# An attention, convolution, expert and MLP model on one core: the order of the first norm tile and kv products, a wait on GpSimd, and twenty-four extra TensorE products

## The reference

```python
def rmsnorm(x, g):
    xf = x * lax.rsqrt(jnp.mean(x * x, axis=-1, keepdims=True) + NORM_EPS)
    return xf * g
...
h = rmsnorm(x, norm1_g)
q, k, v, gate_b, gate_c, xc, ... = split(h @ w_in)     # 512, 128, 128, 512, 512, 512, ...
...
# c_layer of the second block: three branches over the same queries
out = gate0 * o_compressed + gate1 * o_selected + gate2 * o_window
```

## Time and profile before

| | us |
|---|---|
| median of 3 runs | 1994.71 (1994.18 to 1997.05) |
| the profiled execution, its own time | 1996.16 |
| its span, from first to last instruction | 1994.4 |
| TensorE busy in the span | 1874.3 (94%) |
| mean granted TensorE clock | 0.981 |

### The profile page before, as it was taken

The page is one execution under the profiler, slowest core; times in us unless marked ns, Lnnn a source line. Parts: engine busy times, 40 slices in busy tenths (PEclk is TensorE's granted clock), DMA queues, the critical chain, the costliest instruction groups (busy, mean ns, idle before and its releaser), DMA issues.

```text
span 1994.4 us, 28241 instructions
## 1 busy us (share of the span) xinstructions
PE 1874.3 (94%) x11002; PEld 1467.3 (74%) x11002; DVE 1025.2 (51%) x2029; ACT 815.9 (41%) x1551; POOL 565.5 (28%) x401
## 2 busy tenths in 40 slices
PE   6999999998778999988999999999899999999998
PEld 5878889832223893457988888899767798888886
DVE  4170443521113625873376676822567625676777
ACT  4122651311012413364554544353366636544443
POOL 4244431011110420144421123233045643113211
PEclk8999999999889999999999999999889999999999
DMA  6222403799999330201123223321203012223321
GB/s 236 86 85 86 168 1 149 267 401 419 421 420 353 128 107 0 85 1 44 43 100 112 85 85 127 123 71 44 43 2 86 2 43 85 85 85 127 126 85 43
DMA packets 86869, 252.10 MB, mean 126 GB/s; under 512 B 12212, under 2 KB 19700, under 8 KB 74448
## 3 DMA queue, kind: packets, MB, share of 16 engines
q1 hardware_dynamic: 81344, 238.79, 32.5%
q0 software_dynamic: 4592, 9.30, 1.3%
q10 hardware_dynamic: 800, 2.20, 0.3%
HBM read 241.89 MB, written 15.73 MB: 129 GB/s over the span
## 4 chain that ended last, share of the span: by engine, by line
PE 48%; DVE 3%; ACT 3%; issue 2%; POOL 0%; DVEq 0%; ACTq 0%
PE psA L1517 32%; PE psO L2170 2%; PE psO L1686 2%; PE psT L1686 2%; PE psS L1686 2%; PE psT L2211 2%; ACT big L2239 1%; DVE x L2835 1%; PE psA L1635 1%; PE psS L2200 1%; PE psA L2200 1%; PE psO L1583 1%; PE psT L1615 1%; ACT tok L2239 1%; PE psA L2080 1%
## 5 line engine op out<-in xcount | busy, mean ns | idle before, releaser
L1215 POOL TENSOR_TENSOR w_slot<-ring,w_slot 128x1024 fp32r<-128x1024 f32 (+2 forms) x80 | 208.7, 2624 | 539.9 <-ACT w_slot L2239 539.6
L1517 PE MATMUL psA<-hT_hi,w_slot 128*128 128x512 f32 x960 | 297.8, 389 | 0.0
L2239 ACT ACTIVATE w_slot<-ring 128x1024 fp32r<-128x1024 f32 (+2 forms) x178 | 191.9, 1088 | 178.4 <-PE psA L1517 78.4
L1517 PEld LDWEIGHTS psA<-hT_hi,w_slot 128*128 128x128 f32 x960 | 180.2, 188 | 37.2
L2835 DVE TENSOR_TENSOR x<-psA,x 128x512 f32<-128x512 f32 (+1 forms) x206 | 122.4, 623 | 140.1 <-PE psA L1517 135.5
L1517 PE MATMUL psA<-hT_lo,w_slot 128*128 128x512 f32 x480 | 186.7, 389 | 0.0
L2835 DVE TENSOR_TENSOR w_slot<-ring,w_slot 128x1024 fp32r<-128x1024 f32 x98 | 119.9, 1225 | 115.6 <-ACT w_slot L2239 115.6
L2239 ACT ACTIVATE big<-psA 128x512 f32<-128x512 f32 (+7 forms) x145 | 63.9, 465 | 246.1 <-PE psA L1517 141.1
L1517 PE MATMUL psA<-w_slot,hid_part 128*128 128x512 f32 x672 | 161.4, 389 | 0.0
L2239 ACT ACTIVATE scr<-scr,stat 128x384 f32<-128x384 f32 (+3 forms) x224 | 124.4, 556 | 74.1 <-DVE stat L3798 44.4
L1517 PEld LDWEIGHTS psA<-w_slot,hid_part 128*128 128x128 f32 x672 | 126.1, 188 | 26.2
(11 more groups left out here) (465 smaller groups left out, 4491.5 us busy)
## 6 DMA issues: line engine op xcount, KB each, us to landing
ring<-in_mlp_w SPq DMA_DIRECT2D x32, 2048.0 KB, 8.3
ring<-in_w_in SPq DMA_DIRECT2D x8, 2048.0 KB, 8.2
ring<-in_w_gate_e SPq DMA_DIRECT2D x14, 1024.0 KB, 15.7
ring<-in_w_up_e SPq DMA_DIRECT2D x14, 1024.0 KB, 20.8
ring<-in_w_down_e SPq DMA_DIRECT2D x13, 1024.0 KB, 28.3
big<-in_w_down_e SPq DMA_DIRECT2D x12, 1024.0 KB
ring<-in_ab_w_in SPq DMA_DIRECT2D x5, 2048.0 KB, 9.2
scr<-in_w_down_e SPq DMA_DIRECT2D x7, 1024.0 KB
```

Source lines behind the costliest of these rows:

```text
L1215: nc.gpsimd.tensor_tensor(part(w_lo, c), raw_piece(c), part(w_hi, c).bitcast(F32), ALU.subtract)\
L1517: ins = pe.matmul(o, a, b, start=(at == 1), stop=(at == 3 * len(terms)))
L2239: return nc.scalar.activation(o, i, f, **kw)
```

## The change

Three things. The kv product of tile 0 goes back behind the fourth norm tile: TensorE does four norm tiles and then four kv products, with plain job numbers, and ScalarE's and VectorE's parts follow that order. ScalarE copies the gains' vector after all four squares instead of after two. On GpSimd the low part of the second half of the query weights waits until VectorE has written all eight low parts. And in the sparse attention two matmuls whose result nobody reads stand ahead of each of steps 4 to 15.

```diff
-               ("norm0", KD + 1), ("kv", NT - 1), ("q", 2 * NT), ...
+               ("norm0", KD), ("kv", NT), ("q", 2 * NT), ...
...
             for c in range(SPLIT_AT["cp"]):
+                if c == 1:
+                    pool.wait_ge(early_in_lo, KD)
                 split_weight(c)
...
             turn(JOBS["vec"], [vec_rows[:, :]])
-            copied(pe, JOBS["vec"])
-            for t in range(NT - 1):
-                norm_tile(0, t)
+            norm(0)
             need("kv")
             for t in range(NT):
-                o = begin(job("kv", t))
+                o = begin(JOBS["kv"] + t)
...
                 ins.then_inc(proj_ready, 1)
-                if t == 0:
-                    norm_tile(0, NT - 1)
...
+            def beside_first_scores(count):
+
+                for _ in range(count):
+                    pe.matmul(psO[1][:, 0:160], ident, upto[:, 0:160], start=True, stop=True)
+
             def nsa_attention():
 
                 for i in range(n_nsa + VALUE_LAG + AHEAD):
+                    if 4 <= i < MORE_BANKS:
+                        beside_first_scores(2)
...
                 first_root(t)
-                if t == 1:
-                    evac(JOBS["vec"], vec[:, :], 64)
+            evac(JOBS["vec"], vec[:, :], 64)
             copied(act, JOBS["vec"])
             act.wait_ge(const_loaded, CONST_LOADS * 16)
-            for half in range(2):
-                copied(act, norm_turn(0, NT - 2, half))
-            kv_out(0)
             split_weight(SPLIT_AT["q"])
             for half in range(2):
                 copied(act, norm_turn(0, NT - 1, half))
             for k in range(KD):
-                if k == 6:
-                    kv_out(1)
+                if k == 3:
+                    kv_out(0)
                 A(hT_hi_early[:, k, :], hT[:, k, :], ACT.Copy).then_inc(early_in_hi, 1)
+            kv_out(1)
             split_weight(SPLIT_AT["q"] + 1)
...
-            for t in range(NT - 1):
+            for t in range(NT):
                 norm_scale(0, t)
             dve.wait_ge(const_loaded, CONST_LOADS * 16)
             copied(dve, JOBS["vec"])
-            norm_whole(0, 0)
-            norm_scale(0, NT - 1)
-            for t in range(1, NT):
+            for t in range(NT):
                 norm_whole(0, t)
```

More of the change, by code:

```diff
@@ L139 @@
 for _n, _w in (("vec", 1),
-               ("norm0", KD + 1), ("kv", NT - 1), ("q", 2 * NT), ("cc", 4), ("cx", 4), ("cb", 4), ("ga", KD),
+               ("norm0", KD), ("kv", NT), ("q", 2 * NT), ("cc", 4), ("cx", 4), ("cb", 4), ("ga", KD),
                ("gc0", 4), ("gc1", 4), ("mergec", KD), ("mergea", KD), ("wo", 3 * NT), ("tail1", NT + KD),
@@ L172, in job @@
         return JOBS[name] + i - first
-    if stage == "kv":
-        return JOBS["kv"] + i - 1 if i else JOBS["norm0"] + 3 * 2
     if stage == "nk":
@@ L184, in norm_turn @@
         return JOBS[f"tail{n}"] + (3, 6, 8, 11 if n == 4 else 10)[t] + half
-    return JOBS[f"norm{n}"] + 2 * t + half + (n == 0 and t == NT - 1)
+    return JOBS[f"norm{n}"] + 2 * t + half
 APART = {norm_turn(n, t, half): (t, half) for n in (0,) + SPLIT_NORMS for t in range(NT) for half in range(2)}
@@ L309, in weight_plan @@
     w_in = w["w_in"][0]
-    for name, c0, c1, last in (("kv", 512, 768, ("kv", NT - 1)), ("q", 0, 512, "q+7"), ("cc", 1280, 1792, "cc+3"),
+    for name, c0, c1, last in (("kv", 512, 768, "kv+3"), ("q", 0, 512, "q+7"), ("cc", 1280, 1792, "cc+3"),
                                ("cx", 1792, 2304, "cx+3"), ("cb", 768, 1280, "cb+3"),
@@ L2443, in kv_out @@
             def kv_out(t):
-                n = job("kv", t)
+                n = JOBS["kv"] + t
                 product(act, n)
@@ L2896, in norm_whole @@
                     m = norm_turn(n, t, half)
-                    if n in (0, TAIL["mlp0"]) and (t, half) == (NT - 1, 1):
-                        copied(dve, job("nk" if n else "kv", 0))
+                    if n == TAIL["mlp0"] and (t, half) == (NT - 1, 1):
+                        copied(dve, job("nk", 0))
                     if n in SPLIT_NORMS and 2 * t + half >= 6:
@@ L3195, in _ @@
             copied_all(dve, "q", 2 * NT)
-            copied_all(dve, "kv", WIDTH["kv"])
+            copied_all(dve, "kv", NT)
             qk4 = qk.rearrange("p t (h d) -> p (t h) d", d=HD)
```

## The result

The changed kernel takes 1980.55 us (median of 5, 1976.71 to 1982.34) against 1994.71 before (median of 5, 1991.42 to 1997.41); the ratio is 0.9925, 95% interval 0.9909 to 0.9941, so faster by 0.6 to 0.9%. The ratio puts the time at 1979.8, just under the low end of the range. The profiled execution took 1982.04 us, its span is 1980.2: 14.2 under that of before.

A forecast was written before the change was run, and what follows sets the result against it. The prediction took TensorE's own queue to bound the kernel: idle stretches, low clock or added products. Head -11.1 and products 0 took the median 1994.7 to 1983.6 us, range 1980 to 1988.5.

The forecast's parts named there:

- The head, forecast -11.1: First 45 us: first query product starts 9.3 us earlier and regains 1.85 us of low clock, all passed to the end.
- the 1.4 us of room: Before the query products: the last low part is written at 28.5, 1.4 us before TensorE's kv work ends at 29.9.
- The gap, the slow low parts and the late rise: Head, signs of wrong: TensorE gap before first query product; low parts above 0.7 us after GpSimd's first; clock rise after 19.
- Rival 2: Head: low parts stay slow for another reason, such as ScalarE reading the same tiles; gain 2.2, 1992.5 us; chance 0.04.
- Rival 3: Head: part of the new chain is late by 2 to 5 us, such as query weights; 1986 to 1989; chance 0.10.
- the DMA-bound stretch: Full DMA engines at 550 to 600: loads let go by TensorE start earlier, so the whole 11.1 us passes on.
- Rival 1: Head: the clock rises late, kv work ends at 32.0, 2.1 us lost, 1985.7 us; chance 0.07.
- The products, forecast 0: Sparse attention's head: twenty-four unused products, net 0, halfway between clock held (-0.7) and held in part (+1.3).
- the credit for the clock: Sparse attention's head: full clock would save 8.0 of 16.1 busy us, perhaps 4 on the path; 2 if held in part.
- the cost of 3.3: Sparse attention, steps 4 to 15: 24 products take 6.7 us at full clock, half put on the path, +3.3.
- rival 4: Sparse attention: the products keep the clock up throughout; gain 11.1 + 3 or more, 1979 to 1980.6 us; chance 0.09.
- the likely ends of the forecast (-3 to +4): Sparse attention's products: likely ends around the forecast 0; with head 11.1, 1980.6 to 1987.6 us, chance 0.61.

The follow-up runs named there:

- the quarters: The kernel before with GpSimd's first four low parts written as four instructions each, no wait, kv still mid-norm: 1990.79 us, ratio 0.9976.
- the head only: The changed kernel without the twenty-four products: 1982.67 us, ratio 0.9945.
- 22 products by the waits: The changed kernel with 22 products, six ahead of steps 7 and 9, two of 11, 13, 15, one of 5, 6, 16, 17: 1979.8 us.
- one a step: The changed kernel with one product ahead of each of steps 4 to 15 in place of two: 1981.64 us, ratio 0.9936.
- three a step: The changed kernel with three products ahead of each of steps 4 to 15 in place of two: 1984.27 us, ratio 0.9940.
- the head once more: The changed kernel without the twenty-four products, run unaltered again for a second trace: 1985.67 us, ratio 0.9958.
- products only: The kernel before with the twenty-four products alone: 1992.97 us, ratio 0.9991 (0.9979 to 1.0003).
- the changed kernel once more: The changed kernel run unaltered again for a second trace: 1980.62 us, ratio 0.9934.
- order only: The changed kernel without GpSimd's wait and without the products: 1994.06 us, ratio 1.0005.

## Why the prediction came out as it did

**The head, forecast -11.1, measured -11.1 at the first score.** The mechanism was right; that the number fits to the tenth is luck. The nine traces with the new order and the wait have their first score from 1412.6 to 1415.6, against 1426.7 and 1426.1 in the two with the old head, so a pair of traces gives 10.5 to 14.1. Step by step: the low parts ended at 29.0 for 28.5 (the query weights landed at 17.7 for 17.1, and ScalarE and GpSimd passed that on); TensorE's kv work ended at 29.2 for 29.9, so the 1.4 us of room was only about 0.2; the first query copy came at 32.46 for 32.8; GpSimd's second query part from 29.1 to 33.7 was 7 us ahead of its need. The gap, the slow low parts and the late rise that were named as signs of a wrong prediction are absent. That the wait is the cause, and not the order of kv and norm, is shown by doing each alone (10.6 and 0.9 at the first query copy, together the 11.5 of both). That VectorE was held by whole GpSimd instructions is shown by the quarters. Rival 2 falls with both. Rival 3 was near (0.2 us of room): in this trace it didn't come in, and in five of the nine traces with this head TensorE did wait before its first query product, for 0.2 to 0.4 us. The gain did pass through the DMA-bound stretch.

**The clock at the head rose on transposes.** After 9.38 TensorE did nothing but the four tiles' transposes until 15.59. The first three stand 1.7 apart and the fourth takes 1.04 to the next start, so by this spacing the clock had risen within it, before any kv product. The trace of the head only shows it more plainly: its tiles start at 9.17, 10.93, 12.60 and 13.48, the kv products at 14.35, so the last two tiles take 0.87 each, as the one did at full clock before. The column of the granted clock doesn't show the low clock there: it reads 1.00 from the span's start on in these traces, so the spacing is the only evidence. Rival 1 falls, and with it, for these float32 transposes, the sentence of the Trainium skill (TensorE: Matmul & The Clock Gate, Part 4, PE-mode transpose) that full clock doesn't engage for transposes. The measurement decides.

**The products, forecast 0, measured -3.0: the step that failed.** What was mis-sized is the credit for the clock. I counted 4 for a clock held and 2 for one held in part, and took the middle; beside the cost of 3.3 that made 0. The clock was held whole in the profiled execution. A credit of 4 would have given -0.7, so even that was too small. How large it is depends on what the products cost, for which the traces give two readings. The shortest stretch with the clock held is 163.9, with 22 products by the waits. If these cost nothing, the 24 cost 165.4 - 163.9 = 1.5 and the clock gave back 168.4 - 163.9 = 4.5. But twelve products more cost 166.6 - 165.0 = 1.6 where both traces have 10.2 us of low clock (none and one a step), and 167.2 - 165.4 = 1.8 where both have none (two and three a step). By that my estimate for 24 is 3.4, close to the +3.3 of the forecast, and the clock gave back 6.4. So the cost lies between 1.5 and 3.4, the credit between 4.5 and 6.4, out of 20.5 us of low clock; each trace stands for one execution, and which reading is nearer isn't shown. Either way it is rival 4, to which I gave 0.09, and the likely ends of the forecast (-3 to +4) just reach it. No row of before could tell whether the clock would be held, as the prediction says.

**How far this rests on the trace of before.** Without products the low time depends on where the clock falls: 8.7 to 9.0 us after the first score gives 20.5 us of it, 9.7 to 10.0 gives 10.2 and a stretch shorter by 3.5 us. The forecast and the -3.0 both start from a trace of the first kind. Against one of the second (165.0) the products are no gain: with them the stretch is 165.4, 166.1 and 166.6. So what they buy is that the bad case doesn't occur. The seven times of the head once more lie in two groups some 6 us apart. All six traces without products fit such groups (the shorter times have the short case), but the case gives 3.5 of the 6 us; the rest lies elsewhere and isn't shown, and neither is what moves the fall by a us. Over all its runs that kernel has a mean of 1983.2 (13 runs), the changed kernel 1980.4 (11). The difference of -2.8 is uncertain by about 2 us by the scatter of the runs, and products only against before had an interval that includes no change. So the traces show what the products do to the clock; what they are worth in time is shown only roughly.

**The sum.** -11.1 - 3.0 = -14.1 for 14.2 measured in the profiled pair; the ratio's 0.9925 gives -15.0, with an interval from -11.8 to -18.2. The time by the ratio lies 0.2 us under the range; the changed kernel once more, with 0.9934, would lie at 1981.5 and inside it. What is clearly off is the term for the products, not the sum.

## What to carry to other kernels

If a VectorE instruction with two SBUF inputs takes several times its usual duration, look at what GpSimd ran at that moment: here one wait on GpSimd, for work that was still done 7 us before its need, gave back 10.6 us, and rewriting the order of the products gave 0.9. Where TensorE waits in many small pieces and the granted clock falls, products without use can hold it, but they cost TensorE's time too: here they gained some 3 us against the execution with the longest low clock and nothing against the better one. Where single executions of a kernel differ by 6 us, a stretch in the trace between two marks of the program tells more than the span, but it differs between executions as well (165.0 and 168.5 for one kernel), so it takes more than one trace.

## What the runs showed of the hardware that I had not expected

- VectorE and GpSimd took turns by whole instructions, in all lengths tried: a low part of 0.68 us took 4.5 behind a GpSimd part of 4.6, and about 1.75 behind each of seven quarters, the first having taken 1.26. The Trainium skill (GPSIMD Engine Reference, Specifications) speaks of contention with VectorE instructions that have two SBUF inputs, and the traces agree. VectorE's copies out of PSUM weren't held: 0.42 us at 32.46 and 35.31, while GpSimd's parts ran from 29.11 to 38.46, and 0.42 as well at 46.77 in the kernel before, with GpSimd idle.
- GpSimd is slowed in return: two cc parts took 5.53 us while VectorE took turns with them (order only), and 4.75 without (the changed kernel), and eight quarters of the query parts 13.03 us (in quarters).
- Where the clock fell 1 us later within the same work (9.8 us after the first score and not 9.0), the low time was 10.2 us and not 20.5.
